# Layer 0's first four experts loaded at the end of the recurrence, with another order of weight slots

## What is computed

```
for i in range(2):
    h = rmsnorm(x, norm_mix[i])
    x = x + (s5_mixer(h) if i == 0 else nat_mixer(h))        # s5: u = h @ w_in; recurrence both ways; y
                                                             # act = gelu(y); val, gate = split(act @ w_out); val * sigmoid(gate)
    h = rmsnorm(x, norm_ffn[i])
    x = x + sum over e of combine[:, e] * (silu(h @ w_gate[e]) * (h @ w_up[e])) @ w_down[e]      # 32 experts
    gate = sigmoid(rmsnorm(x, norm_ple[i]) @ ple_w_gate[i])
    x = x + gate * (p[i] @ ple_w_proj[i])
```

## Time and profile before

| | |
|---|---|
| time, median of 3 runs | 876.13 us (876.1 to 878.23) |
| profiled execution | 876.75 us, span 875.0 us |
| granted TensorE clock, mean | 0.95 of full speed |
| PE busy | 776.4 us (89%) |
| DVE / ACT / POOL busy | 395.4 / 237.9 / 191.0 us |
| read from HBM | 243.16 MB, 280 GB/s over the span |
| chain that ended last | PE 83%, DVE 7%, issue 5%, ACT 2%, POOL 2%, DMA 1% |

### The profile page before, as it was taken

The page is one execution under the profiler, slowest core; times in us unless marked ns, Lnnn a source line. Parts: engine busy times, 40 slices in busy tenths (PEclk is TensorE's granted clock), DMA queues, the critical chain, the costliest instruction groups (busy, mean ns, idle before and its releaser), DMA issues.

```text
span 875.0 us, 10464 instructions
## 1 busy us (share of the span) xinstructions
PE 776.4 (89%) x3995; PEld 425.9 (49%) x3995; DVE 395.4 (45%) x720; ACT 237.9 (27%) x422; POOL 191.0 (22%) x198
## 2 busy tenths in 40 slices
PE   2667879599999998999999878996999999998997
PEld 1556734543433333346878654545533343333456
DVE  6996742623232322136668658515322232222264
ACT  3323123331111101016575444422310111100153
POOL 5874500221110110000056364002211011010000
PEclk9988979699999999999999959996999999999999
DMA  6035070979999999996787660175199999999761
GB/s 217 1 56 194 5 289 1 390 281 425 421 421 420 421 421 419 422 411 218 260 209 248 250 194 1 54 300 223 57 422 421 420 421 422 421 420 421 321 253 48
DMA packets 61091, 245.46 MB, mean 281 GB/s; under 512 B 19667, under 2 KB 20721, under 8 KB 36081
## 3 DMA queue, kind: packets, MB, share of 16 engines
q1 hardware_dynamic: 56752, 240.36, 69.1%
q0 software_dynamic: 1600, 4.26, 2.1%
q10 hardware_dynamic: 2688, 0.17, 0.2%
HBM read 243.16 MB, written 1.60 MB: 280 GB/s over the span
## 4 chain that ended last, share of the span: by engine, by line
PE 83%; DVE 7%; issue 5%; ACT 2%; POOL 2%; DMA 1%; SPq 0%; ACTq 0%; DVEq 0%; POOLq 0%
PE PS L1794 26%; PE PS L1825 13%; PE PS L1545 10%; PE PS L1835 7%; PE PS L1727 3%; PE PS L2008 3%; PE PS L1765 2%; PE PS L1669 2%; PE PS L1967 2%; PE PS L1988 2%; PE PS L1603 2%; PE PS L1915 2%; PE PS L1806 1%; PE PS L1684 1%; POOL qrs L685 1%
## 5 line engine op out<-in xcount | busy, mean ns | idle before, releaser
L1794 PE MATMUL PS<-ring,xe 128*64 128x512 f32 x1024 | 231.0, 604 | 15.9 <-issue 13.5
L1794 PEld LDWEIGHTS PS<-ring,xe 128*64 128x64 f32 x1024 | 79.8, 139 | 163.7 <-issue 163.7
L1825 PE MATMUL PS<-ring,actT 128*64 128x512 f32 x512 | 116.9, 598 | 1.7 <-DVE actT L1303 1.4
L612 POOL COPY xe<-xg 128x512 f32 x60 | 47.1, 786 | 300.1 <-PE PS L1794 297.7
L1317 DVE TENSOR_TENSOR olo<-PS,ohi 128x512 fp32r<-128x512 f32 x64 | 44.3, 692 | 123.5 <-ACT ohi L855 123.5
L1303 DVE COPY actT<-PS 128x256 f32<-128x256 f32 x32 | 13.6, 425 | 175.6 <-PE PS L1806 175.6
L855 ACT ACTIVATE ohi<-PS 128x512 fp32r<-128x512 f32 x64 | 38.3, 598 | 153.0 <-PE PS L1825 153.0
L1008 DVE SCALAR_TENSOR_TENSOR ringr<-ring,gT,dwh 128x512 fp32r<-128x512 f32 x80 | 62.9, 838 | 26.7 <-ACT dwh L726 25.4
L847 ACT ACTIVATE act<-PS 128x256 f32<-128x256 f32 x32 | 12.3, 385 | 225.5 <-PE PS L1794 225.5
L1825 PEld LDWEIGHTS PS<-ring,actT 128*64 128x64 f32 x512 | 34.7, 136 | 67.1 <-issue 67.1
L1545 PE MATMUL PS<-ringr,rawh 128*128 128x512 f32 x160 | 63.4, 396 | 0.8 <-DVE ringr L1008 0.8
(11 more groups left out here) (323 smaller groups left out, 1031.3 us busy)
## 6 DMA issues: line engine op xcount, KB each, us to landing
ring<-in_moe_w_gate SPq DMA_DIRECT2D x64, 1024.0 KB
ring<-in_moe_w_up SPq DMA_DIRECT2D x64, 1024.0 KB
ring<-in_moe_w_down SPq DMA_DIRECT2D x64, 1024.0 KB, 24.2
ring<-in_nat_w_qkv SPq DMA_DIRECT2D x6, 2048.0 KB
ring<-in_ple_w_gate SPq DMA_DIRECT2D x4, 2048.0 KB
ring<-in_s_w_out SPq DMA_DIRECT2D x2, 2048.0 KB
ring<-in_nat_w_o SPq DMA_DIRECT2D x2, 2048.0 KB
ring<-in_s_w_in SPq DMA_DIRECT2D x1, 2048.0 KB
```

The lines of the kernel that those rows point to most:

```text
L612: pool.tensor_copy(xe[:, e % 4, :, :], xg[:, :, bass.ds(first, CAP)]).then_inc(S("xe_ready"), 1)
L1794: ins = mm(PS[CAP * h_:CAP * h_ + CAP, 0, :].rearrange("p (u f) -> p u f", u=2), xe[:, (2 * p + h_) % 4, k, :], wv[h_][:, k], start=k == 0 ...
L1825: ins = mm(PS[CAP * h_:CAP * h_ + CAP, 2 + n, :], actT[:, k, CAP * h_:CAP * h_ + CAP], wd[h_][:, k, 512 * n:512 * n + 512], start=k == 0, ...
```

## The change

The first six experts of layer 0 get the slots 2, 3, 4, 5, 0, 1 instead of 2, 3, 0, 1, 4, 5, and the wait for `x_ready` ahead of slot 4 goes for layer 0, so that four experts are asked for behind `y_done`. The tiles `ys`, `yT4` and `glu`, which lay in the place of slot 4, get other addresses. The slots of all later loads are turned to match.

```
-        moe_items(0, (2, 3, 0, 1, 4, 5))
-        IT["ple"] = [ple_items(0, 0)]
+        moe_items(0, (2, 3, 4, 5, 0, 1))
+        IT["ple"] = [ple_items(0, 2)]
         wq = I["nat_w_qkv"][0].rearrange("(k p) n -> p k n", p=P)
-        IT["qkv"] = [item((3 + n) % 4, (0, wq[:, :, 512 * n:512 * n + 512])) for n in range(6)]
+        IT["qkv"] = [item((1 + n) % 4, (0, wq[:, :, 512 * n:512 * n + 512])) for n in range(6)]
         wo = I["nat_w_o"][0].rearrange("(k p) n -> p k n", p=P)
-        IT["wo"] = [item((1 + n) % 4, (0, wo[:, :, 512 * n:512 * n + 512])) for n in range(2)]
-        moe_items(1, (3, 0, 4, 5, 1, 2))
-        IT["ple"].append(ple_items(1, 1))
+        IT["wo"] = [item((3 + n) % 4, (0, wo[:, :, 512 * n:512 * n + 512])) for n in range(2)]
+        moe_items(1, (1, 2, 4, 5, 3, 0))
+        IT["ple"].append(ple_items(1, 3))
...
-        ys = at("ys", [P, L, 8, SH], F32, A_XG + 24576)
-        yT = [at(f"yT{n}", [P, SW // P, T], F32, A_XG + 4096 * n) for n in range(5)]
-        glu = [at(f"glu{n}", [P, 512], F32, A_XG + 20480 + 2048 * n) for n in range(2)]
+        ys = at("ys", [P, L, 8, SH], F32, A_H + 8192)
+        yT = [at(f"yT{n}", [P, SW // P, T], F32, A_S if n == 4 else A_XG + 4096 * n) for n in range(5)]
+        glu = [at(f"glu{n}", [P, 512], F32, A_O + 2048 * n) for n in range(2)]
...
                 for e in range(6):
-                    if items[m0 + e][0] == 4:
-                        if i == 0:
-                            sp.wait_ge(S("x_ready"), 1)
-                        else:
-                            sp.wait_ge(S("pv_done"), NH)
+                    if i == 1 and items[m0 + e][0] == 4:
+                        sp.wait_ge(S("pv_done"), NH)
```

## The result

The changed kernel takes 885.06 us (median of 4 runs, 883.76 to 885.4) against 876.12 us (4 runs): ratio 1.0093, 95% interval 1.0075 to 1.0112, 8.9 us slower. In a second series on another chip it was 884.37 against 876.72 us: ratio 1.0084 (1.0067 to 1.0102), 7.7 us. The profiled execution of the first series took 884.75 us (span 883.0), 8.0 us more than that of before.

The account below looks back on a forecast made before the run. Layer 0's expert stage was taken as set by when the unpausing weight stream starts (190.31 us) and whether the loads wanted at its end have landed. 0 + 0 + 5.8 + 1.8 + 0 = +7.6 us gave 883.7 us, range 880.5 to 886.6.

Parts of the forecast that it names:

- Part 1: End of the recurrence: asking for four experts instead of two only lengthens the stream's pause before 190.31 us; 0 us.
- The bound of -9.1 us: Layer 0's expert loop: most the early loads could gain, if all gaps from pair 11 on vanished.
- Part 2: Moved tiles `ys`, `yT4`, `glu`: same instructions, shapes and waits at other addresses; 0 us.
- Part 3, landing: Layer 0's last down projection end (T): TensorE idles until the PLE projection and `p` land; 5.8 us.
- Part 3, cooling: TensorE behind the landing gap: lower clock of 1.2 GHz slows the next matmuls; 1.8 us, bounds 0 and 2.
- The rival without cooling: Wait after layer 0's experts: only the landing costs, no clock lost; 881.9 us, chance 0.17.
- What is late next: Layer 0's PLE gate halves: they land later, but stay hidden before the dense matmuls by 3 to 5 us.
- Part 4: Turned slots of qkv, wo, layer 1's experts and PLE keep their relations: 0 us; the delay reaches the end in full.
- The stream getting ahead: Pairs 11 to 15: early loads remove the gaps (-9.1 us) while the later stall stays; 874.6 us, chance 0.07.
- the projection that isn't waited for: End of layer 0's experts: the PLE projection's slot is free earlier, so no stall; 876.1 us, chance 0.06.
- Late gate halves: Layer 0's dense matmuls: ScalarE's split of the first PLE gate half becomes the bound, 2 us more; 885.7 us, chance 0.06.

Follow-up runs that it names:

- the warmed kernel: Changed kernel plus 48 extra TensorE matmuls in layer 0 between the last down projection and the wait for the PLE projection: 888.16 us, ratio 1.013.
- changed_again: The changed kernel, unedited, run again in the second series on another chip: 884.37 us, ratio 1.0084 against the kernel before.
- late_ple_again: Kernel before with only the changed kernel's later slots (PLE, qkv, w_o, layer 1), second series: 883.43 us, ratio 1.0076.
- short_down: Kernel before with the down matrices of layer 0's experts 6 and 7 loaded to a sixteenth only: 873.55 us, ratio 0.9962.

## Why the prediction was right

**Part 1 (0 us): right.** Two series with the early part alone give ratios of 0.999 and 1.0002. The pause of 6 us became one of 21 (22 forecast), the first gap stayed at pair 11. The bound of -9.1 us had no run to support it. The change gave no slot and took no byte away, and the one run that shortened the loop took bytes away. The Trainium skill ("Perfetto Trace Analysis", Optimization Strategy) says that the same gap, repeated for a stretch on the engine that should be saturated, can mean too little SBUF or PSUM for the next tile. No run here adds a slot, so none shows this for the gaps of 2.02 us; they moved with the bytes, at the same number of slots.

**Part 2 (0 us): right** together with part 1, by the same two runs; the moved tiles alone were not run.

**Part 3, landing (5.8 us): right.** 5.63 us in the profile after, 5.7 in the kernel with the late projection alone. The 5.0 us by the Trainium skill ("DMA: Bandwidth & Descriptors", Anatomy of one DMA) would have been further off; that section gives its figures for one load issued by GpSimd, and here are three, issued by SP.

**Part 3, cooling (1.8 us): right in size, in part by luck.** 13.23 us behind the wait against 11.46 us before are 1.77 us. By the warmed kernel it is 2.31 us of cooling, less 0.54 us of small delays that before has and the warmed kernel hasn't. The prediction had neither: it took over what another gap had cost, and said that nothing would hide it; the two misses nearly cancel. With the landing that is 7.4 us for T to dense (18.86 - 11.46), and 7.65 us between the kernels with the later slots alone and with the early part alone. The rival without cooling (881.9 us) falls: the granted clock behind the wait was 0.50 in both profiles of the changed kernel and in the one with the late slots alone, and with the clock kept at 1.00 the stretch behind the wait took 11.58 instead of 13.48 us.

**What is late next: right, with less cover than it seemed.** I had the first gate half at 11.1 us behind T and hidden by 3 to 5 us. Four profiles have it at 11.2 to 11.3 us. In the changed kernel's first profile it was seen 12.2 us behind T (ScalarE's split began at 411.51), and VectorE's part ended at 415.87, 2.3 us ahead of the dense matmuls. It was hidden there, so the sum stood. In the profile with 22 more matmuls it came at 13.5 us, and TensorE, warm and so earlier at the dense matmuls, waited 0.38 us for it.

**Part 4 and the end.** The delay reached the end, but not "in full" to the tenth. The first profile lost 1.8 us more ahead of T, because the last pair's pass fell to the lower clock (8.79 us at 378.28; in before such a pass fell on an earlier pair, 8.78 us at 363.08, and the next gap took it up: there is none ahead of 377.99), and got 1.2 us back on the way to layer 1's experts. From the table and the two chains: 0.2 (start) + 1.8 + 7.4 - 1.2 - 0.2 (from layer 1's first gate-and-up on) = 8.0 us. So that this profile comes near the forecast of 7.6 us is in part luck: 1.8 and -1.2 us, which the forecast did not have, nearly cancel. The cause of the -1.2 us is not shown; `changed_again` has it too. The medians read 8.9 and 7.7 us, and the executions behind them were profiled only once in each series, so what makes the 1.2 us between the two is not shown.

**The rivals.** The stream getting ahead (874.6 us) falls by the early part alone, the projection that isn't waited for falls by the chain. Late gate halves were no bound in the changed kernel, and one for 0.38 us in the one profile with 22 more matmuls.

## What to carry to other kernels

Before paying for an earlier load, ask what stops the stream next: if it is full buffers, the load only lengthens a pause. When an order of buffers is turned, look up for each later user whose work frees its buffer; here a load that needed pair 13 and now needs pair 15 cost its whole landing, and the clock behind it. So the wait on the engine that bounds the kernel cost more than its length (7.4 us for 5.6).

## What was not expected

- Whether a gap of 2.02 us costs TensorE its clock varies from gap to gap: in before, one of the three in layer 0 was followed by a pass of 8.78 instead of 7.09 us, in the changed kernel two. While the stream is the bound the next gap takes this up; in the last pair it doesn't (+1.7 us).
- In two of the profiles (late_ple_again, short_down) the stretch from the PLE to layer 1's experts took 217.0 and 218.1 us instead of 213 to 214.7. In the first of them score and value matmuls of the attention near 541 us run at about half the rate (2.00 and 1.90 us for four, against 1.07 and 1.01). The granted clock was 0.50 there from 542 to 550 us, and 1.00 in before. In short_down the 4 us lie in the attention too, with a granted clock of 0.50 from 520 to 530 and 0.56 from 530 to 540 us, where before has 0.79 and 1.00. So 4 us of difference between two executions may be clock alone; that all of it is, isn't shown.
- Eight loads of 4 KiB per row, the first four issued into an empty queue, moved 236 and then 265 GB/s in their first 3.5 and next 5 us; four loads of 8 KiB per row moved 290 GB/s in their first 5 us and 415 in the next 5.
